# One hybrid decoder layer: part of the input projection as pairs of seven block products

## The chip, the cores and the metric

The kernel is one program on one core of a Trainium2 chip. The metric is the device time in microseconds, from launch to end. The engines are PE (TensorE, matrix products into eight PSUM banks), DVE (VectorE), ACT (ScalarE), POOL (GpSimd) and SP (SyncE, which here only issues DMAs). Each runs its own instruction list in order and waits on semaphores for the others.

## What is computed

One layer over 1024 tokens of width 1024: modulation from a conditioning vector, a token mixer with two kinds of linear-attention heads, and a squared-ReLU MLP, all in float32.

```
h = modulate(rms_norm(x), shift1, scale1)
proj = h @ w_in                      # 1024 x 3600
gq, gk, gv, g_lr, g_gate, hq, hf, hi, h_gate = split(proj)
# group A: 4 GLA heads (gq, gk, gv, low-rank gate), group B: 4 HGRN2 heads
forget = lb + (1 - lb) * sigmoid(hf)
o_hgrn = chunked_linear_attention(silu(hq), 1 - forget, hi, log(forget), 64)
mixed = concat(rms_norm(o_gla) * silu(g_gate), rms_norm(o_hgrn) * silu(h_gate))
x = x + gate1 * (mixed @ w_out)
h = modulate(rms_norm(x), shift2, scale2)
x = x + gate2 * (square(relu(h @ w_mlp1)) @ w_mlp2)
return rms_norm(x, final_norm_g)
```

A head's attention works on 16 chunks of 64 tokens. Its cumulative sums, exponentials, chunk states and outputs are what the code calls `cum`, `q_rel`, `k_rel`, `k_end`, `state` and `mixed`.

## The kernel before

Activations lie with features on the 128 partitions and tokens along the row: `a_hi` and `a_lo` hold eight tiles of 128 features by 1024 tokens. A float32 number is split into a rounded part and its remainder, so each product takes three matmuls of 512 columns: high weight by high activation, high by low, low by high.

The input projection is cut into units of 128 output columns. `half_unit` (called with the line 1338 of `product`) makes one unit for one half of the tokens: eight tiles times three matmuls, 24 in all, into one of four banks `UB`. Units 0 to 28 are the projection, the rest `w_out`. For each unit SP loads 512 KB (`load_unit`, into `raw`), ACT makes the high part (`high`, line 832), POOL the low part (`low`, line 721).

The units come in groups of four, and between the half-units PE does the attention of the head before (`attention_steps` gives the slots). The groups are `P0` (units 1 to 4) and `P1` (5 to 8) for pairs of GLA heads, `H0` (9 to 12) for the first HGRN head, three passes of `H1` (13 to 24) in a hardware loop for the others, and `G` (25 to 28) for the four HGRN gates. A head's group holds the columns HF, HQ, HI and GG in that order. While group `gi` runs on PE, DVE and ACT turn its columns into forget values, logarithms (`log_a`), the running sum (`cum`, line 2013), its two differences (lines 2015 and 2019), `k_rel` (2024), `k_end` (2026), `q_rel` (2037), `q_cum` (2050). The states (line 1941), masked scores (1921), norms (1949) and remainders of squares (1905) belong to the head before it. In the first groups DVE also adds up the modulation (`ada_acc`, line 1741), whose 48 tiles SP loads among the weights. ACT's function tables are swapped where a logarithm follows another function, as ACT_TABLE_LOAD shows.

The order on every engine is written out by hand. What an engine does first, it does first even if a later item is ready. PE may write a bank only after the reader of its last content has reported; `used` and `unit_read` hold that.

The MLP is already computed with the seven-product scheme of Strassen and Winograd, with weight sums by DVE (`weight_sum`, line 2124), weight remainders by POOL (line 777) and DVE (2145), and ready-made activation operands.

Of the kernel before, what the change touches and what calls it, by code (L numbers as in the profile page):

```python
# [21 lines left out]
F32 = mybir.dt.float32  # L22
# [21 lines left out]
U_OUT = 29  # L44
U_MLP = 37
# [16 lines left out]
BLOCK_ORDER = (3, 0, 1, 2)  # L62

# [92 lines left out]
def attention_steps(own, prev):  # L156
# [4 lines left out]
    s = [[] for _ in range(8)]  # L161
# [11 lines left out]
    if prev == "H":  # L173
        s[0] += [("k", 0, 0, 0)]
        s[1] += [("up", 0, 0, 2), ("up", 1, 0, 3), ("sc", 0, 0, 1)]
        s[2] += [("k", 0, 1, 0), ("sc", 0, 1, 1)]
        s[3] += [("o", 0, 0, 2)]
        s[4] += [("up", 2, 1, 3), ("up", 3, 1, 0), ("ss", 0, 0, 1)]
        s[5] += [("o", 0, 1, 2)]
        s[6] += [("ss", 0, 1, 3)]  # L180
# [5 lines left out]
    if own in "PH":  # L186
        s[7] += [("v", 0, 0, 0), ("v", 0, 1, 1)]
# [44 lines left out]
def chunks_after(prev, q):  # L232
# [7 lines left out]
IN_TURN = ((0, 0), (0, 1), (1, 0), (1, 1))  # L240
BY_HALVES = ((0, 0), (1, 0), (0, 1), (1, 1))
# [7 lines left out]
            for n in range(48)]  # L249


def hybrid_layer(nc, x, c, w_ada, b_ada, w_in, gate_w2, gate_b2, gla_g, lb_logits, hgrn_g, w_out, w1, w2,
# [3 lines left out]
    with ExitStack() as ctx:  # L256
# [61 lines left out]
        shift_gap = at("shift_gap", 206.6875, [P, KH])  # L318
        hid_dram = nc.dram_tensor("hidden_scratch", [4, 7, P, KH, HALF], F32, kind="Internal").ap()
# [75 lines left out]

        def tok(t, half):
            return t[:, half * HALF:(half + 1) * HALF]
# [14 lines left out]
        def at_chunk(pos):  # L412

            return chunked(cum)[:, :, pos:pos + 1].broadcast_to([P, NC, CH])
# [16 lines left out]
        MB = [[UB[2], UB[1], UB[0], UB[3]], [SB[0], SB[3], SB[1], SB[2]]]  # L431
        OB = (UB[2], UB[0], UB[3], UB[1])
# [35 lines left out]
        def groups(e, group):  # L468
# [4 lines left out]
            with e.Fori(1, 4) as h:  # L473
                group("H1", h + 2, h)
            group("G", 6, None)
# [38 lines left out]
        def _(sp):  # L514
# [44 lines left out]
            for j, q in enumerate(pair_cols + head_cols):  # L559
                load_unit(2 + j, j % 2, w_in, 0, q)  # L560
                for _ in range((2, 2, 5, 3, 4, 3, 3, 4, 2, 0, 0)[j]):
                    load_ada(n)
                    n += 1
            with sp.Fori(1, 4) as h:
                for j, q in enumerate(head_cols):
                    load_unit(4 * h + 9 + j, (1 + j) % 2, w_in, 0, h * P + q)
            for h in range(4):
                load_unit(25 + h, (1 + h) % 2, w_in, 0, HG + P * h)

            def load_out(v):  # L570

                if v >= 2:
                    sp.wait_ge(wlo_out, v - 1)
                else:
                    sp.wait_ge(wlo_ready, U_OUT + v - 1)
# [53 lines left out]
            for v in range(4):  # L629
# [1836 lines left out]
```

## Time and profile before

| | |
|---|---|
| median of three runs | 1174.47 us (1173.69 to 1175.45) |
| profiled execution, first to last instruction | 1173.7 us |
| PE busy | 1154.4 us, 98% |
| DVE, ACT, POOL busy | 807.6, 597.9, 444.0 us |
| stretch of the loop of heads and the gates on PE | 226.6 to 451.7 us |
| data moved | 152 MB |

The profile shows one execution, and its span lies 0.8 us under the median of the runs. In its rows a time is in us unless it is marked ns; "idle before" is time in which the engine waited, with the instruction that released it. The duration of a matmul includes its way through the array: matmuls overlap, and the pace of a series is the distance of their starts.

### The profile page before, as it was taken

Reading aid. Unit: us, or ns where it says so; the run is one execution under the profiler, and the core shown is the slowest. Engines: PE = TensorE matmul, PEld = TensorE weight load, DVE = VectorE, ACT = ScalarE, POOL = GpSimd, SP = SyncE. Lnnn points to the kernel's source line nnn. Section 1 sums busy time; section 2 is a strip of 40 time slices with the busy share of each in tenths; the row PEclk is TensorE's granted clock in tenths of the full one; section 3 lists DMA queues with packets and bytes.
Section 4 is the critical chain, followed back from the end, with each engine's and each line's share of the span. In section 5 each row is a group of like instructions: output and inputs, shape, how many; then the busy total and the mean of one; then the engine's idle time right before and its main releaser. Section 6 shows DMA issues by size and latency. Waiting matters only on the chain.

```text
span 1173.7 us, 15673 instructions
## 1 busy us (share of the span) xinstructions
PE 1154.4 (98%) x5651; PEld 958.1 (82%) x5651; DVE 807.6 (69%) x958; ACT 597.9 (51%) x899; POOL 444.0 (38%) x274
## 2 busy tenths in 40 slices
PE   7999999999999999999999999999999999999997
PEld 6788788888888888888888888888878888888886
DVE  6898766554536358367987755676796784966776
ACT  7763554646464647235655555455663443434325
POOL 1021111111111115326444442435367574666751
PEclk9899999999999999999999999999999999999999
DMA  9765241021111114341455435534723737437203
GB/s 351 261 224 171 90 145 36 18 55 36 36 36 36 37 38 143 90 161 72 117 171 165 158 118 171 179 135 130 220 72 118 251 98 253 151 123 280 92 1 144
DMA packets 148765, 152.02 MB, mean 130 GB/s; under 512 B 6228, under 2 KB 117976, under 8 KB 146008
## 3 DMA queue, kind: packets, MB, share of 16 engines
q1 hardware_dynamic: 148696, 151.12, 39.7%
q8 instruction: 41, 0.67, 0.2%
q14 instruction: 28, 0.23, 0.1%
HBM read 117.02 MB, written 34.08 MB: 129 GB/s over the span
## 4 chain that ended last, share of the span: by engine, by line
PE 91%; DVE 3%; issue 2%; DMA 2%; SPq 1%; ACT 1%; DVEq 0%; ACTq 0%
PE unit_bank L1338 33%; PE unit_bank L1640 8%; PE unit_bank L1642 8%; PE unit_bank L1641 8%; PE small_bank L1642 8%; PE small_bank L1640 8%; PE small_bank L1641 8%; PE small_bank L1338 3%; PE small_bank L1473 2%; DMA ada_slot<-in_w_ada_dram 2%; PE small_bank L1377 1%; PE small_bank L1465 1%; DVE ada_acc L1741 1%; DVE state L1941 1%; DVE op_lo L2254 0%
## 5 line engine op out<-in xcount | busy, mean ns | idle before, releaser
L777 POOL TENSOR_TENSOR wr_lo<-quarter,wr_hi 128x512 fp32r<-128x512 f32 x122 | 196.2, 1622 | 175.0 <-ACT wr_hi L1130 174.9
L1338 PE MATMUL unit_bank<-a_hi,w_hi 128*128 128x512 f32 x560 | 223.7, 400 | 0.0
L1338 PE MATMUL unit_bank<-a_hi,w_lo 128*128 128x512 f32 x560 | 218.7, 391 | 0.0
L1338 PE MATMUL unit_bank<-a_lo,w_hi 128*128 128x512 f32 x560 | 218.5, 390 | 0.0
L721 POOL TENSOR_TENSOR w_lo<-raw,w_hi 128x1024 fp32r<-128x1024 f32 x27 | 67.7, 2506 | 348.5 <-ACT w_hi L832 348.5
L1640 PE MATMUL unit_bank<-op_hi,wr_hi 128*128 128x512 f32 x452 | 176.6, 391 | 0.7 <-DVE op_lo L2254 0.6
L1642 PE MATMUL unit_bank<-op_hi,wr_lo 128*128 128x512 f32 x452 | 176.0, 389 | 0.0
L1641 PE MATMUL unit_bank<-op_lo,wr_hi 128*128 128x512 f32 x452 | 175.9, 389 | 0.0
L1640 PE MATMUL small_bank<-op_hi,wr_hi 128*128 128x512 f32 x448 | 174.6, 390 | 0.0
L1642 PE MATMUL small_bank<-op_hi,wr_lo 128*128 128x512 f32 x448 | 174.4, 389 | 0.0
L1641 PE MATMUL small_bank<-op_lo,wr_hi 128*128 128x512 f32 x448 | 174.4, 389 | 0.0
L1130 ACT ACTIVATE wr_hi<-wr_full 128x512 fp32r<-128x512 f32 x90 | 56.8, 631 | 176.2 <-DVE wr_full L2124 173.1
L2124 DVE TENSOR_TENSOR wr_full<-quarter,quarter 128x512 f32<-128x512 f32 x90 | 87.9, 977 | 57.6 <-PE unit_bank L1642 25.6
L1130 ACT ACTIVATE wr_hi<-quarter 128x512 fp32r<-128x512 f32 x136 | 82.7, 625 | 85.9 <-PE unit_bank L1642 47.4
L1338 PEld LDWEIGHTS unit_bank<-a_hi,w_hi 128*128 128x128 f32 x560 | 105.5, 188 | 23.0 <-issue 2.1
L1338 PEld LDWEIGHTS unit_bank<-a_hi,w_lo 128*128 128x128 f32 x560 | 105.4, 188 | 22.7
L1338 PEld LDWEIGHTS unit_bank<-a_lo,w_hi 128*128 128x128 f32 x560 | 105.6, 189 | 21.5 <-issue 0.7
L777 POOL TENSOR_TENSOR wr_lo<-wr_full,wr_hi 128x512 fp32r<-128x512 f32 x48 | 80.5, 1680 | 77.1 <-ACT wr_hi L1130 48.0
L1640 PEld LDWEIGHTS unit_bank<-op_hi,wr_hi 128*128 128x128 f32 x452 | 84.9, 188 | 19.0 <-issue 1.7
L1641 PEld LDWEIGHTS unit_bank<-op_lo,wr_hi 128*128 128x128 f32 x452 | 84.8, 188 | 17.8 <-issue 0.2
L1642 PEld LDWEIGHTS unit_bank<-op_hi,wr_lo 128*128 128x128 f32 x452 | 84.9, 188 | 17.7
L1641 PEld LDWEIGHTS small_bank<-op_lo,wr_hi 128*128 128x128 f32 x448 | 84.2, 188 | 17.5
(273 smaller groups left out, 1856.3 us busy)
## 6 DMA issues: line engine op xcount, KB each, us to landing
quarter<-in_w_mlp_dram SPq DMA_DIRECT2D x128, 256.0 KB, 4.4
hidden_scratch<-hid SPq DMA_DIRECT2D x98, 256.0 KB, 2.9
ada_slot<-in_w_ada_dram SPq DMA_DIRECT2D x48, 512.0 KB, 5.5
op_full<-hidden_scratch SPq DMA_DIRECT2D x21, 1024.0 KB, 4.9
raw<-in_w_in_dram SPq DMA_DIRECT2D x29, 512.0 KB, 3.8
raw<-in_w_out_dram SPq DMA_DIRECT2D x16, 512.0 KB, 4.0
x_stage<-in_x_dram SPq DMA_DIRECT2D x8, 512.0 KB, 5.1
x_scratch<-xT SPq DMA_DIRECT2D x2, 2048.0 KB, 8.3
```

The source lines that it names most:

```text
L721: pool.tensor_tensor(w_lo[slot][:, :, :], raw[slot][:, :, :], w_hi[slot][:, :, :].bitcast(F32), ALU.subtract).then_inc(wlo_ready, 1)
L777: pool.tensor_tensor(wr_lo[slot][:, :, :], split_source(n), wr_hi[slot][:, :, :].bitcast(F32), ALU.subtract).then_inc(wr_lo_pool, 1)
L1130: act.activation(wr_hi[slot][:, :, :], split_source(n), ACT.Copy).then_inc(wr_hi_ready, 1)
L1338: return pe.matmul(out_ap, left, right, start=start, stop=stop)
L1377: mm = pe.transpose(SB[b][:, i * P:(i + 1) * P], tile, ident[:, :])
L1465: pe.matmul(SB[b][:, i * P:(i + 1) * P], v_nat[:, which, 4 * half + i, :], masked[:, slot, i * P:(i + 1) * P], start=i == 0, stop=False, s ...
L1473: mm = pe.matmul(SB[b][:, c * CH:(c + 1) * CH], state[mine, n, :], q_cum[mine, n * CH:(n + 1) * CH], start=False, stop=c == 7, skip_group_ ...
L1640: pe.matmul(dst, wh, ah, start=opens, stop=False, skip_group_check=True)
L1641: pe.matmul(dst, wh, al, start=False, stop=False, skip_group_check=True)
L1642: mm = pe.matmul(dst, wl, ah, start=False, stop=k == KH - 1, skip_group_check=True)
L1741: dve.scalar_tensor_tensor(acc, src, col(cond, k), acc, ALU.mult, ALU.add).then_inc(ada_added, 1)
L2124: dve.tensor_tensor(dst[:, :, :], a[:, :, :], b[:, :, :], op).then_inc(w_sum, 1)
```

## The change

From the second HGRN head on (groups `H1` and `G`) the 16 units become 8 pairs of units. A pair is a matrix of two units by two halves of the features, multiplied with two halves of the features by two halves of the tokens, by seven block products instead of eight. A product has four tiles (12 matmuls). P1, P2, P6, P5, P4 and P3 run as wholes, P7 as four pieces of three matmuls between them.

- Activation sums are made once, in group `H0`, over xT's place after x has been stored to DRAM (8 DMAs): POOL does eight additions and subtractions and two remainders, each of 128x2048; ACT four high parts, DVE two remainders. The operand of P7 goes to DRAM and comes back for each pair in pieces.
- Weight sums of a pair: S3 and S2 by DVE, S1 and S4 by POOL. High parts by ACT (seven of 128x512 instead of two of 128x1024), low parts all by POOL.
- The results: ACT copies twice out of PSUM (`copy_part`), DVE does five additions (`join`) per pair. Columns are paired as (HQ, HF) and then (GG, HI) for a head.
- The hardware loop over three heads is written out. The order of the operations of a head on DVE and ACT is new, and PE's attention slots in it are nine instead of eight. The two half-units of unit 12 are swapped.
- Before `w_out`, x (4 MB) and one tile of `mixed` are loaded back. The first half of the output projection takes the tiles in another order, and the banks `MB` and `OB` change order.

The core of the diff:

```diff
@@ groups @@
-            with e.Fori(1, 4) as h:
-                group("H1", h + 2, h)
-            group("G", 6, None)
+            for h in range(1, 4):
+                paired(h + 2, h)
+            gates(6)
@@ gpsimd @@
-            for u in range(2, 13):
+            def add_parts(dst, k, half, n):
+                if n:
+                    pool.wait_ge(t_made, T_MADE_0 + n)
+                pool.tensor_tensor(dst[:, :, :], blocks(a_hi, k, half).bitcast(F32), blocks(a_lo, k, half).bitcast(F32), ALU.add
+                                   ).then_inc(t_made, 1)
...
+            for u in range(2, 10):
                 low(u, u % 2)
-            with pool.Fori(0, 4) as i:
-                for j in range(4):
-                    low(4 * i + 13 + j, (1 + j) % 2)
+            pool.wait_ge(x_out, X_OUT_0 + 16 * KT)
+            pool.wait_ge(lo_dve, 16)
+            add_parts(xs[1], 0, 1, 0)
+            add_parts(xs[0], 1, 1, 1)
+            subtract(xs[3], xs[0], xs[1], 2)
+            low(10, 0)
+            pool.wait_ge(t_high, T_HIGH_0 + 1)
+            pool.tensor_tensor(t3_lo[:, :, :], xs[3][:, :, :], t3_hi[:, :, :].bitcast(F32), ALU.subtract).then_inc(t_made, 1)
+            low(11, 1)
+            pool.wait_ge(t3_stored, T3_STORED_0 + 32)
+            add_parts(xs[2], 0, 0, 4)
+            subtract(xs[1], xs[1], xs[2], 5)
+            low(12, 0)
+            subtract(xs[3], xs[0], xs[1], 6)
+            add_parts(xs[0], 1, 0, 7)
+            subtract(xs[2], xs[0], xs[3], 8)
+            pool.wait_ge(t_high, T_HIGH_0 + 2)
+            pool.tensor_tensor(t1_lo[:, :, :], xs[1][:, :, :], t1_hi[:, :, :].bitcast(F32), ALU.subtract).then_inc(t_made, 1)
+            for p in range(PAIRS):
+                for prod in SPLIT_ORDER:
+                    if prod in (P5, P3):
+                        late_weight_sum(p, prod)
+                    pair_low(p, prod)
@@ scalar, group H0 @@
+                    act.wait_ge(t_made, T_MADE_0 + 9)
+                    act.activation(t1_hi[:, :, :], xs[1][:, :, :], ACT.Copy).then_inc(t_high, 1)
@@ scalar, paired @@
+                forget_tanh(0, early, "21")
+                output(0)
+                act.wait_ge(hk_ready, h + 1)
+                act.activation(t0[:, :], t0[:, :], ACT.Ln).then_inc(log_a, 1)
+                act.wait_ge(filled["sc"], before("sc", gi + 1))
+                tanh_of(q_rel, 1, early, "12")
+                pair_high(late, P6)
...
+                tanh_of(t0, 0, late, "11")
+                pair_high(late + 1, P1)
+                norm(1)
+                act.wait_ge(filled["o"], before("o", gi + 1))
+                value_of(1, late, "22")
+                pair_high(late + 1, P7)
+                pair_high(late + 1, P2)
+                value_of(0, late, "21")
@@ tensor @@
+            def seventh_piece(p, j):
+                if j == 0:
+                    pe.wait_ge(pair_lo, PAIR_LO_0 + split_of(p, P7))
...
+                        pe.wait_ge(c_read["12"], C_READ_0["12"] + p)
...
+                pair_product(early, P4)
+                attend(4)
+                pair_product(early, P3)
+                pair_product(late, P1)
+                attend(5)
+                seventh_piece(late, 0)
+                pair_product(late, P2)
...
+                pair_product(late, P4)
+                pair_product(late, P3)
+                if name == "H1":
+                    attend(8)
@@ vector, paired @@
+                join(early, "12")
+                dve.wait_ge(log_a, gi + 1)
+                dve.tensor_tensor_scan(own_cum[:, :], carry[:, :], t0[:, :], 0.0, ALU.mult, ALU.add).then_inc(cum_ready, 1)
+                dve.wait_ge(cum_ready, gi + 1)
+                dve.tensor_tensor(chunked(t0), chunked(own_cum), at_chunk(CH // 2 - 1, own_cum), ALU.subtract).then_inc(d_mid, 1)
...
+                dve.tensor_tensor(chunked(k_end), chunked(own_cum), at_chunk(CH - 1, own_cum), ALU.subtract).then_inc(d_last, 1)
+                silu_of(q_rel, 1, early, "12", made + 2)
+            def silu_of(dst, half, p, c, n):
+                dve.wait_ge(tanh_ready, TANH_0 + n)
+                wait_quarter(dve, p, c)
+                dve.scalar_tensor_tensor(tok(dst, half), tok(dst, half), 1.0, quarter_bank(p, c), ALU.add, ALU.mult).then_inc(c_read[c], 1)
@@ sync @@
+            load_out(0)
+            load_mixed_back()
+            load_out(1)
+            for i in range(2):
+                load_x_back(i)
+            for v in range(2, 4):
                 load_out(v)
```

## Rows read from the trace of the kernel before

**Rows 1.** The page: busy time of each engine, then the chain by engine.

```profile
PE 1154.4 (98%) x5651; PEld 958.1 (82%) x5651; DVE 807.6 (69%) x958; ACT 597.9 (51%) x899; POOL 444.0 (38%) x274
...
PE 91%; DVE 3%; issue 2%; DMA 2%; SPq 1%; ACT 1%; DVEq 0%; ACTq 0%
```

**Rows 2.** Stretch: us, busy PE, PEld, DVE, ACT, POOL, clock, DMA share, GB/s.

```profile
234.00:451.00 217.00, 216.53 (x1180) 181.75 (x1179) 111.51 (x142) 117.93 (x163) 42.71 (x19) 1.00 0.14 39
```

**Rows 3.** The chain of waits in that stretch: start us, us, what.

```profile
247.61 5.47 PE unit_bank L1338 x24
```

**Rows 4.** Timeline of POOL: start us, us, line, operation, [idle before and releaser].

```profile
145.71 2.40 POOL L721 TENSOR_TENSOR w_lo<-raw,w_hi 128x1024 fp32r<-128x1024 f32 x1 [11.50 <-ACT w_hi L832]
...
296.43 2.39 POOL L721 TENSOR_TENSOR w_lo<-raw,w_hi 128x1024 fp32r<-128x1024 f32 x1 [6.81 <-ACT w_hi L832]
```

**Rows 5.** Timeline of DVE in the same two places.

```profile
146.97 3.42 DVE L1741 SCALAR_TENSOR_TENSOR ada_acc<-ada_slot,misc,ada_acc 128x1024 f32<-128x1024 f32 x2
150.31 1.21 DVE L2037 SCALAR_TENSOR_TENSOR q_rel<-t,q_rel 128x1024 f32<-128x1024 f32 x1
...
156.65 1.30 DVE L1905 TENSOR_TENSOR sq_lo<-stat,sq_hi 128x512 fp32r<-128x512 f32 x2 [4.25 <-ACT sq_hi L1004]
...
174.76 0.70 DVE L2010 TENSOR_SCALAR t<-t 128x1024 f32<-128x1024 f32 x1
...
296.52 2.85 DVE L2010 TENSOR_SCALAR t<-t 128x1024 f32<-128x1024 f32 x1
```

**Rows 6.** POOL and DVE timelines in the MLP, both always with work.

```profile
623.97 1.74 POOL L777 TENSOR_TENSOR wr_lo<-quarter,wr_hi 128x512 fp32r<-128x512 f32 x1
624.48 1.77 DVE L2124 TENSOR_TENSOR wr_full<-quarter,quarter 128x512 f32<-128x512 f32 x1
625.67 1.74 POOL L790 TENSOR_TENSOR hid<-hid,hid1B 128x512 f32<-128x512 f32 x1
626.29 1.67 DVE L2124 TENSOR_TENSOR quarter<-quarter,wr_full 128x512 f32<-128x512 f32 x1
```

**Rows 7.** All instructions of POOL's line 777 in the trace: min/median/max ns.

```profile
L777 POOL TENSOR_TENSOR wr_lo<-quarter,wr_hi x122: 1271/1299/2987, 534.4 to 1128.6; 128x512 fp32r<-128x512 f32 x122
```

**Rows 8.** Timeline of PE at the end of P1 and in H0.

```profile
159.44 0.39 PE L1338 MATMUL small_bank<-sq_hi,ones 128*128 128x512 f32 x1
...
207.13 1.13 PE L1338 MATMUL small_bank<-v_nat,k_nat 64*128 64x256 f32 x6
```

**Rows 9.** Timeline of DVE in H0.

```profile
198.51 1.23 DVE L2019 TENSOR_TENSOR t<-cum 128x1024 f32<-128x1024 f32 x1 [4.04 <-ACT k_rel L1073]
199.66 1.22 DVE L2024 TENSOR_TENSOR k_rel<-k_rel,t 128x1024 f32<-128x1024 f32 x1
200.92 1.23 DVE L2026 TENSOR_TENSOR k_end<-k_end,t 128x1024 f32<-128x1024 f32 x1
```

**Rows 10.** Timeline of ACT in H0: it releases banks.

```profile
205.56 1.27 ACT L997 ACTIVATE stat<-small_bank,misc 128x512 f32<-128x512 f32 x2
```

**Rows 11.** Groups of DVE and ACT in one head, 302 to 359 us: busy us, mean ns.

```profile
L2013 DVE TENSOR_TENSOR_SCAN cum<-carry,t 128x1024 f32<-128x1024 uint8 x1 | 2.3, 2276 | 0.0
...
L1065 ACT ACT_TABLE_LOAD x1 | 1.3, 1283 | 0.0
```

**Rows 12.** Timeline of ACT: one norm of a head and its end.

```profile
331.51 1.28 ACT L997 ACT_TABLE_LOAD   x1
333.66 0.69 ACT L997 ACTIVATE stat<-small_bank,misc 128x512 f32<-128x512 f32 x1 [0.86 <-PE small_bank L1338]
...
336.20 1.07 ACT L957 ACTIVATE vT<-unit_bank 128x512 f32<-128x512 f32 x2
```

**Rows 13.** The page: DMA issues, KB each, median us to landing.

```profile
quarter<-in_w_mlp_dram SPq DMA_DIRECT2D x128, 256.0 KB, 4.4
...
x_scratch<-xT SPq DMA_DIRECT2D x2, 2048.0 KB, 8.3
```

**Rows 14.** A stretch near 48 us, columns as in rows 2.

```profile
48.00:50.00 2.00, 2.00 (x6) 1.55 (x5) 2.00 (x6) 2.00 (x4) 0.00 (x0) 0.50 1.10 384
```

More of the change, by code:

```diff
@@ L466, in h_place, with groups @@
             return (((P1, P2), (P6, P3))[half][k // KH], k % KH)
-        def groups(e, group):
+        def groups(group, paired, gates):
             group("P0", 0, None)
@@ new lines, in load_mixed_back, with load_x_back @@
+            def load_mixed_back():
+                sp.wait_ge(seventh_done, SEVENTH_0 + 4 * PAIRS - 1)
+                sp.dma_start(mixed[:, 0, :], mixed_dram).then_inc(mixed_back, 16)
+            def load_x_back(i):
+                sp.wait_ge(six_done, six_of(PAIRS - 1, P4 if i else P5))
+                for half in range(2):
+                    part = slice(half * HALF, (half + 1) * HALF)
+                    sp.dma_start(xT[:, 4 * i:4 * i + 4, part], x_dram[:, 4 * i:4 * i + 4, part]).then_inc(x_back[i][half], 16)
@@ L766, in _ @@
+            for half in range(2):
+                low_tiles(mixed, a_hi, a_lo, half)
+            pool.wait_ge(gated, 12)
             pool.memset(t1[:, :], 0.0).then_inc(sum2, 1)
@@ L1100, in inverse_rms @@
+            groups(group, paired, gates)
             def inverse_rms(half):
@@ L1566, in _, with stage @@
-            groups(pe, group)
+                    stage(name, steps[name][jj], used, gi, u0)
+            def stage(name, pieces, used, gi, u0):
+                prev = GROUPS[name][1]
+                older = {"P0": [], "P1": ["P0"], "H0": ["P1"], "H1": ["H0"] if gi == FIRST_PAIRED else ["H1"], "G": ["H1"]}[name]
+                both = []
+                for p in pieces:
+                    b = p[3]
+                    if name == "P0" and p[0] == "z" and p[2] == 1:
+                        half_unit(u0 + 1, 2, 0, a_hi, a_lo, tiles=range(KH))
+                    if b in used:
+                        pe.wait_ge(read[used[b][0]], reads(prev, used[b], gi))
+                    elif name == "P0":
+                        kind, count = (("ada", 3), ("ada", 4), ("ada", 1), ("ada", 2))[b]
+                        pe.wait_ge(read[kind], count)
+                    else:
+                        for name_ in older:
+                            kind = [q for x in steps[name_] for q in x if q[3] == b][-1][0]
+                            pe.wait_ge(read[kind], before("chunks" if kind == "up" else kind, gi))
+                    used[b] = p
+                    if p[0] not in ("sc", "up", "o"):
+                        step(prev, p, gi, u0)
+                        continue
+                    both.append(p)
+                    if len(both) == (2 if prev == "P" or p[0] == "up" else 1):
+                        {"sc": scores, "up": updates, "o": outputs}[p[0]](prev, both, gi)
+                        both = []
@@ L1568, in out_unit, with paired, gates @@
+            def paired(gi, h):
+                two_pairs("H1", gi)
+            def gates(gi):
+                two_pairs("G", gi)
+            groups(group, paired, gates)
             def out_unit(v):
@@ L2060, in scale_half @@
+            groups(group, paired, gates)
             def scale_half(half, k):
```

786 lines of the change are left out of this document (650 added, 136 removed).

## Prediction, made before the kernel was built

> **What bounds the kernel now.** I read the page first: PE is busy 98% of the span, and the chain that ended last is 91% PE [rows 1]. Then the stretch that the change rewrites, 226.6 to 451.7 us: of 217 us of it PE is busy 216.5, at the full clock, with POOL busy 43, DVE and ACT 112 and 118 [rows 2]. So matmuls taken out there are worth their whole time, and every new wait of PE costs its whole length. The chain of waits gives the pace: a half-unit of 24 matmuls takes 5.47 us [rows 3], 0.228 us each. The 32 half-units are 175 us of the 225; the other 50 are the attention of four heads, 12.6 us each. Last I read POOL beside DVE, since the change moves most of its preparation to POOL, and PE, DVE and ACT where PE has least slack.
>
> **What the change removes.** 16 units are 768 matmuls, 8 pairs of 7 products of 12 are 672. 96 x 0.228 = 21.8 us less on PE. Attention keeps its instructions, so this is the most that can be won: 5.5 us a head.
>
> **GpSimd against VectorE.** Two places show one rule. At 296.43 POOL starts a remainder of 2.39 us; DVE starts L2010 0.09 us later and takes 2.85 us, where the same instruction takes 0.70 at 174.76 [rows 4, 5]. It ended 0.55 after POOL. At 145.71 the same happens to an addition to `ada_acc`: the two take 3.42 us, 1 us too long [rows 4, 5]. Where both engines always have work they take turns: each DVE instruction of 0.69 takes 1.7, each of POOL's of 1.3 takes 1.74 [rows 6, 7]. So a DVE instruction with two operands in SBUF waits for the whole POOL instruction that is running, and POOL waits for DVE's. DVE instructions that read a PSUM bank show no such waiting in these views, so the new joins are safe. In the paired groups POOL's instructions are 1.3 us, and DVE loses up to 1.3 at each meeting. In H0 they are 128x2048, which this trace has none of. From 1.30 us at 512 columns and 2.40 at 1024 [rows 4, 7] each further 512 cost 1.1, so 2048 cost 4.6 us; bounds are 2.4 (no dearer than the longest seen) and 5.2 (four times 1.3). Ten of these are 46 us. The Trainium skill (GPSIMD Engine Reference, section 3.1) measures a `tensor_tensor` addition of 2048 fp32 elements at 4497 ns on GpSimd and 2293 on VectorE, and advises VectorE for elementwise work; by it the ten would be 45 us, and the change goes against that advice. No run here shows it yet.
>
> **End of P1, 7.6 us.** POOL is free after the weights of unit 9, at 148.1 us [rows 4], and x has long been stored: SP issues those eight DMAs near 105 us into an idle queue, so they cost nothing. POOL then runs three of the long instructions with no wait between. DVE has there, in order, the second addition to `ada_acc`, `q_rel`, five tiny ones and then the remainders of the squares, which begin at 156.65 and take 1.30 [rows 5]. Taking turns: POOL 149.2 to 153.8, addition to 155.0, POOL to 159.5, `q_rel` to 160.7, POOL to 165.2, the tiny ones, the remainders 166.1 to 167.4. PE wants the first sum of squares at 159.44 [rows 8] and gets it near 167. Bounds: 0 if POOL doesn't hold DVE, 9 if also the tiny ones are held singly. I take 7.6.
>
> **Middle of H0, 11.4 us.** After the store of P7's operand (2 MB, 8.3 us [rows 13], done near 197) POOL has six long ones and one of 2.4, of which five fall into the path of `k_end`. DVE's L2019, L2024 and L2026 run back to back before, 198.51 to 202.1 [rows 9]. With PE 8.2 us later, L2019 comes at 206.7 and waits 2.2, L2024 waits 4.6, L2026 4.6: 11.4 late. Behind L2026 stands ACT: it reads unit 10's banks, then the sums of squares at 205.56 [rows 10], and PE waits with the updates at 207.13 [rows 8] for exactly that bank. Before, the slack is 0.3 us, so all 11.4 go through. The swapped unit 12 waits for the same reads. Bounds 0 and 16.
>
> **First pair, 4 us.** ACT's high part of t1 waits for POOL's ninth result (226.2 us by the same turns), and behind it on ACT stand the squares, vT and the high parts of the first pair. The last reader of unit 12, which P2 waits for, comes after a norm (3.8 us without its wait [rows 12]). I get P2 about 4 us late; bounds 0 and 8.
>
> **Three heads, 16.5 us.** Steady state, two waits.
> First, piece 0 of the late P7 waits until DVE has read quarter 12 (`c_read["12"]`). Count from the end of the early P3. PE wants the piece after P1 (2.73) and the updates and sums (1.1 + 0.5 [rows 8]): at 4.1. The output bank is filled at -2.7; ACT takes three of 0.54 [rows 12] for it, a table load of 1.28 [rows 11] and the logarithm of 1.06: 1.2. DVE's scan takes 2.3 [rows 11], two differences 1.15 each as L2019 to L2024 [rows 9], the product 0.6: 6.5. That is 2.4 late, and 3.7 if POOL's low part of P6 falls between the differences, which it does by my count. I take 3.2.
> Second, the transposes of v. Count from the end of the late P6; PE is ready for them at 10.3. S4 on POOL comes behind a low part and a norm of DVE, done at 3.0. Only then may SP load the next first quarter (4.4 us [rows 13], 3.0 to 4.4 in this quiet queue): 6.7. ACT has that high part, a norm of 3.8, and four of 0.5 before it hands over the last half of v: 13.0. So 2.7 late. With 0.3 for P3, a head waits 6.2 us. My sums have attention at 12.1 us where it took 12.6 to 12.9, so 0.7 is absorbed: 5.5 a head, 16.5 for three. That eats the 5.5 that a head wins. Bounds 0 and 9 a head.
> The written-out loop takes branch gaps from DVE, none of which PE waits for: 0.
>
> **Gates and the way into w_out, 3.4 us.** The gates have no scan, and no wait of PE comes out at P7. But 4 MB of x and one tile of `mixed` come back ahead of the third and fourth `w_out` tile on one queue. At twice the 8.3 us for 2 MB [rows 13] they land 17 us after the last P5, unit 2 of `w_out` gets its weights 2.5 late, and the second 0.9. Bounds 0 and 8. New bank orders in the MLP change no count: 0.
>
> **Sum.** -21.8 + 7.6 + 11.4 + 4 + 16.5 + 3.4 = +21.1 us. On the profiled span of 1173.7 that is 1194.8, and with the 0.8 around it 1195.6 us.
>
> **Rivals.**
> A. The schedule holds: POOL's long instructions let DVE through and the two waits of a head are hidden; PE keeps its pace. For it: on average every engine has room (POOL 9 x 1.3 of 25 us a pair). Against: rows 4 to 6, and 0.3 us of slack in H0. Time 1174.5 - 21.8 = 1152.7, up to 1165 with small waits.
> B. Only POOL's hold in H0 is wrong (long instructions are cut into pieces, or POOL finds gaps): the heads still wait. 1174.5 - 21.8 + 16.5 + 3.4 + 3 = 1175.6, between 1168 and 1186.
> C. Slower still: PE's clock. After light use PE runs at 0.50 of its clock, 1.2 GHz, at 48 us: 6 starts in 2 us [rows 14], near 0.43 us a matmul instead of 0.228, 1.8 us for nine. If each of the three long waits and of some eight shorter ones is followed by that, it adds up to 11 x 1.8 = 20: 1205 to 1216. It decides from the point where a wait of PE is long enough to lower the clock; the stretches at full clock have none. The Trainium skill (TensorE: Matmul & The Clock Gate, "HAM oscillation") says that idle gaps between bursts send the array back to 1.2 GHz; by it the three long waits at least, 5 us, belong on top, 1200.6. No wait of several us stands in the trace to confirm it.
> That the kernel doesn't do what it says: 96 matmuls fewer is countable; if products were done anew, it would show as more matmuls. I give it nothing.
>
> **Chances.** Forecast (1186 to 1205) 0.44, A 0.16, B 0.22, C 0.16, outside 0.02. The range from 1167 to 1212 takes the forecast, B and most of C, and leaves A out. A measurement of this kernel can tell 0.2% from no change, 2.3 us. Faster by more (under 1172.1): A and a third of B, 0.23. Within: 0.09. Slower: 0.68.
>
> **What would show it.** Right: PE idle 7 us at the sums of squares near 159 us, with DVE's L1905 ending there; POOL instructions of 4.6 us; `k_rel` and `k_end` products of over 5 us in H0; in each head a gap of PE of 2 to 4 us ahead of the first P7 piece of the late pair, released by DVE's product on quarter 12, and one ahead of the v transposes, released by ACT. Wrong: DVE's two-operand instructions of 1.2 us beside a long POOL one; PE without gaps between 226 and 440 us. The prediction fails most easily at the hold of the long instructions (19 us of it rest on it), next at the order in which ACT gets through a head.

## Result and profile after

The changed kernel takes 1220.89 us (median of four runs, 1216.72 to 1222.83) where the kernel before takes 1174.5: the ratio is 1.0394, 95% interval 1.0374 to 1.0414. It is slower, by 46 us where 21 were forecast, and it lies above the predicted range (1212). The profiled execution spans 1219.2 us, 45.5 more than before.

The page, busy time by engine with the number of instructions, and the shares of the chain that ended last (compare [rows 1]):

```profile
PE 1155.1 (95%) x5555; PEld 952.6 (78%) x5555; DVE 884.2 (73%) x1023; ACT 621.4 (51%) x939; POOL 560.4 (46%) x340
...
PE 79%; DVE 7%; issue 4%; ACT 4%; DMA 3%; POOL 2%; SPq 1%; DVEq 0%; ACTq 0%; POOLq 0%
```

These two lines already hold the result. PE has the 96 matmuls less that were promised (5651 to 5555), worth 21.8 us, and yet it is busy 0.7 us longer: 22.5 us went mostly into slower matmuls. The clock accounts for 20.6 of them: from the first wait on PE is busy for 41.1 us while the granted clock is at the lower of its two levels, and half of such time is lost (0.43 us a matmul for 0.228); the kernel before is never busy at that level behind 60 us. The other 1.9 us are not placed. PE's idle time, span less busy, grew from 19.3 to 64.1 us: 44.8. So 45.5 = 44.8 of waits + 22.5 of slower matmuls - 21.8.

By stretch (us, then busy PE, PEld, DVE, ACT, POOL, the granted clock, DMA share, GB/s), to be held against [rows 2]:

```profile
161.00:175.00 14.00, 9.30 (x40) 7.83 (x41) 11.63 (x15) 6.93 (x10) 3.56 (x2) 0.76 0.35 112
...
200.00:240.00 40.00, 30.45 (x175) 23.89 (x171) 28.10 (x27) 17.96 (x23) 28.46 (x7) 0.87 0.11 34
...
325.00:387.00 62.00, 56.18 (x295) 46.37 (x296) 39.73 (x52) 35.23 (x52) 26.51 (x19) 0.92 0.37 115
387.00:448.00 61.00, 55.05 (x280) 45.39 (x278) 39.34 (x51) 35.09 (x52) 25.66 (x19) 0.92 0.35 102
448.00:490.00 42.00, 41.98 (x237) 35.40 (x236) 30.39 (x45) 25.88 (x40) 21.06 (x16) 1.00 0.52 165
```

The loss sits at the end of P1, in H0, in the first pair and in each of the heads. The gates (448 to 490) run without a wait and at the full clock. A head takes 61.2 us (transposes of v at 315.24, 376.34, 437.72) where it took 56.6 (282.36, 338.90, 395.49).

**The first head.** POOL and DVE at the end of P1, and POOL with DVE in H0 (compare [rows 4, 5, 9]):

```profile
147.49 11.08 POOL L976 TENSOR_TENSOR x_sum<-a_hi,a_lo 128x2048 f32<-128x2048 f32 x2
158.65 5.36 POOL L982 TENSOR_TENSOR x_sum<-x_sum,x_sum 128x2048 f32<-128x2048 f32 x1
...
183.68 4.63 POOL L1013 TENSOR_TENSOR t_lo<-x_sum,t_hi 128x2048 fp32r<-128x2048 f32 x1 [6.84 <-ACT t_hi L1299]
```

```profile
154.01 5.64 DVE L2557 SCALAR_TENSOR_TENSOR q_rel<-t,q_rel 128x1024 f32<-128x1024 f32 x1
159.57 4.45 DVE L2334 TENSOR_TENSOR misc<-misc 128x4 f32<-128x4 f32 x1
164.06 0.18 DVE L2335 RECIPROCAL misc<-misc 128x4 f32<-128x4 f32 x1
...
208.65 5.62 DVE L2544 TENSOR_TENSOR k_rel<-k_rel,t 128x1024 f32<-128x1024 f32 x1
214.20 5.54 DVE L2546 TENSOR_TENSOR k_end<-k_end,t 128x1024 f32<-128x1024 f32 x1
```

A product of DVE that takes 1.2 us takes 5.6 beside POOL's long instructions, and one of four columns takes 4.45, until POOL's third sum ends at 164.0. PE's timeline shows the two waits (in brackets, with the releaser) and what follows the second (compare [rows 8]):

```profile
165.70 0.77 PE L1775 MATMUL small_bank<-sq_hi,ones 128*128 128x512 f32 x1 [6.70 <-DVE sq_lo L2448]
...
224.51 2.04 PE L1775 MATMUL small_bank<-v_nat,k_nat 64*128 64x256 f32 x6 [9.30 <-ACT stat L1268]
226.48 1.97 PE L1814 MATMUL small_bank<-ident,ada_acc 128*128 128x128 f32 x8
228.10 0.77 PE L1775 MATMUL unit_bank<-a_hi,w_hi 128*128 128x512 f32 x1
228.67 0.63 PE L1775 MATMUL unit_bank<-a_lo,w_hi 128*128 128x512 f32 x1
229.10 0.63 PE L1775 MATMUL unit_bank<-a_hi,w_lo 128*128 128x512 f32 x1
```

After the wait the updates take 2.04 us instead of 1.13 and matmuls start 0.43 us apart instead of 0.23; the granted clock from 224 to 230 us is 0.50, 1.2 GHz, the lower of the two levels.

**The heads.** DVE and PE at the P7 piece of the first paired head:

```profile
284.85 2.29 DVE L2713 TENSOR_TENSOR_SCAN cum<-carry,t 128x1024 f32<-128x1024 uint8 x1
287.18 1.23 DVE L2715 TENSOR_TENSOR t<-cum 128x1024 f32<-128x1024 f32 x1
288.32 2.29 DVE L2718 TENSOR_TENSOR k_end<-cum 128x1024 f32<-128x1024 f32 x1
290.54 0.68 DVE L2632 SCALAR_TENSOR_TENSOR q_rel<-q_rel,unit_bank 128x512 f32<-128x512 f32 x1
```

```profile
291.32 0.47 PE L2056 MATMUL unit_bank<-piece_x,pw_hi 128*128 128x512 f32 x1 [3.22 <-issue]
```

The chain of waits just before the transposes of v (start, us, what):

```profile
302.81 1.31 POOL pw_full L993
...
304.14 4.29 DMA pair_quarter<-in_w_in_dram
...
308.51 0.63 ACT pw_hi L1359
...
309.16 1.28 ACT L1389
...
312.46 0.63 ACT stat L1391
...
314.61 0.50 ACT vT L1419
...
315.24 1.34 PE small_bank L1814 x8
```

All PE waits over 0.2 us between 100 and 520 us make 44.3 us (the rows are rounded one by one):

| place, prediction's step | measured | in the sum |
|---|---|---|
| end of P1 | 6.7 | 7.6 |
| middle of H0 | 9.3 | 11.4 |
| first pair (0.26, 1.76, 4.14, 1.70) | 7.9 | 4 |
| three heads: P7 pieces 3 x 3.2, transposes of v 2.5, 2.6, 2.7 | 17.5 | 16.5 |
| way into w_out (0.56, 0.52, 1.88) | 3.0 | 3.4 |
| matmuls slower than 0.228 us | 22.5 | 0 |

The sum of the waits was forecast to within 1.4 us (42.9), in part by luck, since the first pair came out 3.9 us too long and H0 2.1 too short; the heads, the largest term, were right to 1 us. Nearly the whole miss is the last line.

### The profile page after: what moved, and what is told of

The parts are those of the page before. It is cut to its first block, busy times and chain, and to the rows that moved or that the text cites. A ratio compares the mean times of both kernels' runs of the same rounds, so it can differ in the third digit from the quotient of the medians.

```text
span 1219.2 us, 15677 instructions
## 1 busy us (share of the span) xinstructions
PE 1155.1 (95%) x5555; PEld 952.6 (78%) x5555; DVE 884.2 (73%) x1023; ACT 621.4 (51%) x939; POOL 560.4 (46%) x340
## 4 chain that ended last, share of the span: by engine, by line
PE 79%; DVE 7%; issue 4%; ACT 4%; DMA 3%; POOL 2%; SPq 1%; DVEq 0%; ACTq 0%; POOLq 0%
PE unit_bank L1775 14%; PE unit_bank L2181 8%; PE unit_bank L2183 8%; PE unit_bank L2182 8%; PE small_bank L2181 8%; PE small_bank L2183 8%; PE small_bank L2182 8%; PE small_bank L1775 2%; PE unit_bank L2036 2%; PE unit_bank L2037 2%; PE unit_bank L2038 2%; POOL pw_lo L1001 2%; DVE ada_acc L2282 1%; DMA ada_slot<-in_w_ada_dram 1%; PE small_bank L1912 1%
## 5 line engine op out<-in xcount | busy, mean ns | idle before, releaser
L1775 PE MATMUL unit_bank<-a_hi,w_hi 128*128 128x512 f32 x304 | 122.9, 404 | 1.9 <-DVE w_lo L2426 1.9
L1775 PE MATMUL unit_bank<-a_lo,w_hi 128*128 128x512 f32 x304 | 119.9, 394 | 0.0
L1775 PE MATMUL unit_bank<-a_hi,w_lo 128*128 128x512 f32 x304 | 119.6, 393 | 0.0
L2181 PEld LDWEIGHTS small_bank<-op_hi,wr_hi 128*128 128x128 f32 x448 | 84.1, 188 | 17.5 <-POOL wr_lo L1043 0.2
L2183 PEld LDWEIGHTS small_bank<-op_hi,wr_lo 128*128 128x128 f32 x448 | 84.1, 188 | 17.6
L936 POOL TENSOR_TENSOR w_lo<-raw,w_hi 128x1024 fp32r<-128x1024 f32 x11 | 27.7, 2515 | 121.5 <-ACT w_hi L1098 121.5
L1001 POOL TENSOR_TENSOR pw_lo<-pair_quarter,pw_hi 128x512 fp32r<-128x512 f32 x32 | 48.7, 1522 | 72.5 <-ACT pw_hi L1359 72.5
```

Of the source, the lines that this page charges most:

```text
L936: pool.tensor_tensor(w_lo[slot][:, :, :], raw[slot][:, :, :], w_hi[slot][:, :, :].bitcast(F32), ALU.subtract).then_inc(wlo_ready, 1)
L1001: pool.tensor_tensor(pw_lo[place][:, :, :], pair_source(prod), pw_hi[place][:, :, :].bitcast(F32), ALU.subtract).then_inc(pair_lo, 1)
L1775: return pe.matmul(out_ap, left, right, start=start, stop=stop)
L2181: pe.matmul(dst, wh, ah, start=opens, stop=False, skip_group_check=True)
L2183: mm = pe.matmul(dst, wl, ah, start=False, stop=k == KH - 1, skip_group_check=True)
```

## Experiments

The theory is the table: DVE held behind POOL's instructions, two waits in every head by the order on DVE and on ACT, and behind every wait a stretch at the lower clock. The rivals are named with each run. The span is that of the profiled execution. "Idle" is the span less PE's busy time; "slow" is busy time less 1154.4 plus 0.2275 us for every matmul fewer than 5651. It holds the price of the lower clock and 1.5 to 5 us besides, and it comes from one execution.

| kernel | median us | ratio to before (95%) | span | idle | slow |
|---|---|---|---|---|---|
| changed | 1220.9 | 1.0394 (1.0374 to 1.0414) | 1219.2 | 64.1 | 22.5 |
| 1 sums in column tiles | 1209.2 | 1.0308 (1.0291 to 1.0326) | 1204.5 | 53.0 | 18.9 |
| 2 sums in halves, a single execution | 1214.2 | | 1212.5 | 61.8 | 18.1 |
| 3 added matmuls in the waits | 1208.2 | 1.0305 (1.0286 to 1.0324) | 1206.1 | 50.2 | 9.0 |
| 4 ScalarE's order | 1210.5 | 1.0307 (1.0282 to 1.0331) | 1208.7 | 59.7 | 16.4 |
| 5 VectorE's order | 1220.2 | 1.0402 (1.0385 to 1.0419) | 1217.6 | 62.2 | 22.8 |
| 6 VectorE's order and states | 1221.5 | 1.0419 (1.0401 to 1.0436) | 1218.2 | 65.4 | 20.2 |
| 7 P2 ahead of the P7 piece | 1216.4 | 1.0380 (1.0361 to 1.0398) | 1211.5 | 61.1 | 17.8 |
| 8 runs 1, 4, 6 together | 1196.8 | 1.0204 (1.0187 to 1.0221) | 1196.8 | 49.8 | 14.4 |
| 9 runs 1, 4 together | 1197.2 | 1.0204 (1.0187 to 1.0221) | 1196.5 | 48.4 | 15.5 |
| 10 as 9, P2 ahead of the P7 piece | 1196.3 | 1.0207 (1.0189 to 1.0225) | 1193.4 | 50.2 | 10.6 |
| 11 as 9, added matmuls | 1195.0 | 1.0182 (1.0165 to 1.0199) | 1193.8 | 39.6 | 10.7 |

Differences of a few us need care. The kernel before was run again beside every set: its median was 1174.5 us beside the changed kernel and 1172.7 to 1173.3 beside the others, so across sets the ratios are the fair measure. By them runs 1, 3 and 4 gained 10.1, 10.4 and 10.2 us where the medians give 11.7, 12.7 and 10.4. And PE reaches its first wait, ahead of which no edit has changed its work, between 157.0 and 159.0 us in these profiles: before 60 us it is busy at the lower clock for 6.8 us in the changed kernel and in runs 1, 4 and 6, for 3.4 in 5, 7, 8 and 9, for 10.2 in 11 and not at all in 2, 3 and 10. So what a run changed is read from its own stretch.

### 1. GpSimd's ten long instructions in column tiles

```diff
-                pool.tensor_tensor(dst[:, :, :], a[:, :, :], b[:, :, :], ALU.subtract).then_inc(t_made, 1)
+                for j in range(KH):
+                    ins = pool.tensor_tensor(dst[:, j, :], a[:, j, :], b[:, j, :], ALU.subtract)
+                ins.then_inc(t_made, 1)
```

> The ten GpSimd instructions of 128x2048 are issued as four of 128x512 each; everything else is as changed. Theory (a VectorE instruction with two SBUF operands waits for the whole GpSimd instruction in front of it): each turn costs VectorE 1.3 us instead of 4.6, so PE's gap of 6.7 us at the sums of squares near 159 us falls under 2, that of 9.3 us near 215 us under 4, and with the slow matmuls behind them 13 to 17 us are won: 1204 to 1208 us. Rival (what counts is GpSimd's work as a whole, not the length of one instruction): the sums take as long or longer, and the time stays within 3 us of 1220.9.

Measured 11.7 us less where 13 to 17 were expected: the theory's direction, 1.2 us above its range. DVE in this kernel, at the two places shown above:

```profile
149.45 2.28 DVE L2561 SCALAR_TENSOR_TENSOR q_rel<-t,q_rel 128x1024 f32<-128x1024 f32 x1
151.65 1.25 DVE L2338 TENSOR_TENSOR misc<-misc 128x4 f32<-128x4 f32 x1
...
163.38 1.26 DVE L2573 COPY decay<-cum 128x16 f32<-128x16 f32 x1
...
202.13 2.30 DVE L2548 TENSOR_TENSOR k_rel<-k_rel,t 128x1024 f32<-128x1024 f32 x1
204.35 2.30 DVE L2550 TENSOR_TENSOR k_end<-k_end,t 128x1024 f32<-128x1024 f32 x1
```

The same work on the same data in shorter instructions holds DVE 1.1 us at a time, not 4.4. The wait near 159 us falls from 6.7 to 0.99, the one in the middle of H0 from 9.3 to 2.68, with a new one of 1.81 at 181.6. What is left over in the first pair (2.44, 4.02, 0.85) and in the heads stays. So the hold is by instruction, and these waits were its doing. The COPY at 163.38 has one operand and 16 columns and takes 0.17 us in the changed kernel (at 168.47); here, beside POOL's third sum, it takes 1.26. So some instructions with one operand are held too.

### 2. The same ten in halves

```diff
-                for j in range(KH):
-                    ins = pool.tensor_tensor(dst[:, j, :], a[:, j, :], b[:, j, :], op)
+                for j in range(0, KH, 2):
+                    ins = pool.tensor_tensor(dst[:, j:j + 2, :], a[:, j:j + 2, :], b[:, j:j + 2, :], op)
```

> The ten long GpSimd instructions as two of 128x1024 each. PE's gap near 159 us was 6.7 us with 128x2048 and 1.0 us with 128x512. Theory (a VectorE instruction waits for one GpSimd instruction, here 2.4 us): about 3 us there, with a time between 1209 and 1221 us, near 1213. Rival (the hold is not set by the length of one instruction): a gap like one of the two others.

For 2048, 1024 and 512 columns the wait in H0 is 9.3, 5.3 and 2.7 us (at 1024 with a further one of 2.4 at 228.1), but the one at the end of P1 is 6.7, 6.2 and 1.0. That is a miss: 3 us were expected there, and the rival had it, a gap like that of the whole sums. Only the time (1214.2 for some 1213, from one execution) came as expected. DVE and POOL of this kernel say why:

```profile
149.92 3.38 DVE L2561 SCALAR_TENSOR_TENSOR q_rel<-t,q_rel 128x1024 f32<-128x1024 f32 x1
153.22 2.37 DVE L2338 TENSOR_TENSOR misc<-misc 128x4 f32<-128x4 f32 x1
155.62 0.18 DVE L2339 RECIPROCAL misc<-misc 128x4 f32<-128x4 f32 x1
155.84 2.08 DVE L2340 TENSOR_TENSOR misc<-misc 128x4 f32<-128x4 f32 x1
157.96 0.17 DVE L2342 TENSOR_SCALAR misc<-misc 128x4 f32<-128x4 f32 x1
158.16 2.18 DVE L2343 TENSOR_TENSOR misc<-misc 128x4 f32<-128x4 f32 x1
160.38 3.40 DVE L2452 TENSOR_TENSOR sq_lo<-stat,sq_hi 128x512 fp32r<-128x512 f32 x2
```

```profile
157.98 4.64 POOL L974 TENSOR_TENSOR x_sum<-x_sum,x_sum 128x1024 f32<-128x1024 f32 x2
```

DVE has seven instructions with two SBUF operands there, three of them of four columns, and each waits for one of POOL's. Whole sums (three) or halves (six) both last DVE until POOL is done, at 164.0 and 162.6; with twelve quarters DVE gets through first. In these three kernels the price of holding is about the smaller of POOL's remaining work and DVE's instructions times POOL's length. In H0 only three of DVE's stand in the path, so there the length decides.

### 3. Matmuls without use in the two waits of a head

```diff
                 attend(5)
+                if name == "H1":
+                    pe.wait_ge(read["o"], before("o", gi) + 1)
+                    keep_warm(2, 12)
                 seventh_piece(late, 0)
...
                 if name == "H1":
+                    pe.wait_ge(read["up"], before("chunks", gi) + 15)
+                    keep_warm(0, 9)
                     attend(8)
```

`keep_warm` issues matmuls of 512 columns into a bank that is free and isn't read before it is overwritten.

> In each of the three heads PE does 12 extra matmuls of 512 columns ahead of the first P7 piece of the late pair and 9 ahead of the v transposes, into a bank that is free there, with results that nobody reads. They fill 2.7 of the 3.2 us and 2.0 of the 2.5 us that PE waits. Theory (a wait costs its length and then a run of matmuls at half clock, which the trace shows as 6 to 12 starts 0.43 us apart): the waits stay where they end, the slow runs behind them go, 10 to 14 us less: 1207 to 1211 us. Rival (the slow matmuls have another cause, and PE's work in the gap only adds): 1221 us or more.

PE does 63 matmuls more and the kernel is 12.7 us faster. The page, PE at the P7 piece, and the stretches of the last two heads:

```profile
PE 1155.9 (96%) x5618; PEld 954.1 (79%) x5618; DVE 882.4 (73%) x1023; ACT 620.7 (51%) x939; POOL 560.7 (46%) x340
```

```profile
286.24 2.90 PE L2071 MATMUL small_bank<-a_hi,ones 128*128 128x512 f32 x12
289.66 0.47 PE L2056 MATMUL unit_bank<-piece_x,pw_hi 128*128 128x512 f32 x1 [0.52 <-issue]
```

```profile
325.00:387.00 62.00, 60.49 (x328) 50.47 (x328) 40.22 (x54) 36.66 (x54) 28.87 (x20) 1.00 0.40 122
387.00:448.00 61.00, 59.56 (x327) 49.72 (x326) 42.05 (x55) 35.67 (x52) 27.61 (x19) 1.00 0.39 119
```

The clock is 1.00 where it was 0.92. In the changed kernel PE is busy for 24.7 us at the lower level between 290 and 445 us, in the three heads; here it never is, and half of that, 12.4 us, is what the clock cost there, most of the 16.4 that three seven-product heads save. The rest agrees: the added matmuls take 14.3 us and the waits in the heads shrink by 13.0, so that a head should be 3.7 us shorter, and it takes 57.5 us instead of 61.2. "Slow" falls by 13.5 over the whole kernel, but part of that lies before 60 us, where nothing was edited.

### 4. ScalarE's order: the norm ahead of a high part that waits for a load

```diff
-                pair_high(late + 1, P1)
                 norm(1)
+                pair_high(late + 1, P1)
```

> ScalarE does the second norm of a head ahead of the high part of the next pair's P1, which waits for a load. Theory (the chain S4 on GpSimd, load of 4.3 us, high part, norm of 3.8 us, copies of v holds PE's v transposes): the load is now hidden by the norm, the three gaps of 2.6 us and the slow matmuls behind them go, 4 to 4.5 us a head, 1207 to 1209 us. Rival (the copies are late because ScalarE has too much to do, not because it waits for the load): under 3 us in all.

10.4 us less, 1.5 us above the expected range. The wait at v falls from 2.5 to 2.7 us to 1.33 in each head, and "slow" by 6.1. The predicted chain (S4, load, high part, norm, v) is confirmed in part: take the load out from before the norm, and half the wait goes, where all of it was expected to. The rest hangs on ACT's high part of P1, POOL's low part, DVE's second sum and the addition before v's last copy: four steps on three engines.

### 5. VectorE's order: quarter 12 directly behind the scan

```diff
+                silu_of(q_rel, 1, early, "12", made + 2)
                 dve.wait_ge(cum_ready, gi + 1)
                 dve.tensor_tensor(chunked(t0), chunked(own_cum), at_chunk(CH // 2 - 1, own_cum), ALU.subtract).then_inc(d_mid, 1)
...
                 dve.tensor_tensor(chunked(k_end), chunked(own_cum), at_chunk(CH - 1, own_cum), ALU.subtract).then_inc(d_last, 1)
-                silu_of(q_rel, 1, early, "12", made + 2)
```

> VectorE reads quarter 12 (the product for q_rel) right after the running sum and ahead of the two differences. Theory (the first P7 piece of the late pair waits for that read alone): the three gaps of 3.2 us and the slow matmuls behind them go, 5 us a head, about 1205 us. Rival (the piece waits for GpSimd's low part of P6, which the chain of waits names in front of it): the gaps stay and the time is 1221 us.

A miss: 0.7 us, which is nothing (ratios 1.0402 and 1.0394). The waits at P7 are gone, and three of 2.69 to 2.79 us stand at the outputs with the states, which DVE's line 2659 releases behind the same two differences:

```profile
287.57 2.32 DVE L2719 TENSOR_TENSOR k_end<-cum 128x1024 f32<-128x1024 f32 x1
...
290.94 2.64 DVE L2659 SCALAR_TENSOR_TENSOR state<-state,decay,small_bank 128x128 f32<-128x128 f32 x7
```

```profile
293.63 3.68 PE L1912 MATMUL small_bank<-q_cum,state 128*128 128x64 f32 x16 [2.69 <-DVE state L2659]
```

The outputs then take 3.68 us at the low clock where 2.00 us are shown for them at the high one in run 10 below, so that the clock costs as much as before ("slow" 22.8 for 22.5).

### 6. The states moved forward too

```diff
                 dve.tensor_tensor(chunked(t0), chunked(own_cum), at_chunk(CH // 2 - 1, own_cum), ALU.subtract).then_inc(d_mid, 1)
+                states(1)
...
                 dve.tensor_tensor(k_rel[:, :], k_rel[:, :], t1[:, :], ALU.mult).then_inc(k_rel_ready, 1)
-                states(1)
```

> As the run before with quarter 12 read right after the running sum, and now the second half of the states stands between the two differences instead of behind the product for k_rel. In that run the wait at the P7 piece was gone, but PE waited 2.7 us for those states at the outputs of the second half. Theory (two waits stood behind one another, the second hidden by the first): both go now, 3 x (3.2 + some 2 of slow matmuls), 1203 to 1207 us. Rival (a third wait of the same size stands behind, since VectorE is short of time in this half of a head): 1215 to 1221 us.

The rival had it: 1221.5. Both waits are gone; new ones of 3.16, 1.29 and 3.15 us stand at the second sum of squares, one of 1.54 behind the transfer of a P7 piece, and those of v grow to 3.66 and 4.56 (the third is 1.93). The reading that fits is that DVE as a whole is behind PE at this point of a head and that its order only chooses who waits; no run took work away from DVE, so it isn't shown by itself.

### 7. On PE, P2 of the late pair ahead of the first P7 piece

```diff
-                seventh_piece(late, 0)
                 pair_product(late, P2)
+                seventh_piece(late, 0)
                 seventh_piece(late, 1)
```

> The changed kernel with the new place of P2 alone (P2 of the late pair ahead of the first P7 piece). Theory of the single wait: 3 x 1.8 us of waits and 3 x (1.5 to 2.4) us of slow matmuls go, if the transposes of v don't take it: 1209 to 1212 against 1220.9. Rival: in the changed kernel the transposes of v stand behind ScalarE, whose norm waits for the high part of P1's next sum and that for a transfer (4.3 us), a chain that starts from PE's progress only in part; PE then waits 4 us instead of 2.6 there and two thirds of the gain are lost: 1216 to 1220.

1216.4: the rival had the time (1216 to 1220), if not quite the place. By the medians that is 4.5 us less, by the ratios 1.6 with overlapping intervals, so a gain is not shown. In the profile, an execution at the fast end (1213.5), the P7 waits fall from 3.2 to 0.53 us, but the outputs with the states wait 1.64 and v 2.7 to 3.0, where the rival had all of it at v: of 8.1 us of idle time 5.6 come back in the heads. It is "slow" that falls more, by 4.7.

### 8. Runs 1, 4 and 6 in one kernel

The edits of runs 1, 4 and 6, and in H0 ACT's two copies of the tanh ahead of t4's high part:

```diff
-                    act.wait_ge(t_done, T_DONE_0 + 1)
-                    act.activation(t4_hi[:, :, :], xs[2][:, :, :], ACT.Copy).then_inc(t_high, 1)
                     act.wait_ge(q_cum_ready, gi + 1)
                     tanh_and_copy(3, (1, 0))
+                    act.wait_ge(t_done, T_DONE_0 + 1)
+                    act.activation(t4_hi[:, :, :], xs[2][:, :, :], ACT.Copy).then_inc(t_high, 1)
```

> The GpSimd sums as four instructions of 128x512, the norm of ScalarE ahead of the high part of P1, VectorE's order as in e5, and unit 12 read ahead of the high part of t4. Theory (waits and the slow matmuls behind them are separate places on PE's path, so their shares add): 11.7 + 10 + 15 + 3 us off 1220.9: 1178 to 1184 us. Rival (they share slack on ScalarE and VectorE, so one mended place gives way to the next): 1190 us or more.

The rival again: 1196.8, as the shares don't add. The first pair shows 2.46, 2.27 and 3.47 us, the last one now behind the transfer of a P7 piece; the second sums of squares still wait 3.04, 1.31 and 3.12.

### 9. The same without VectorE's new order

> The combined version without the new order of VectorE's instructions: GpSimd's ten long instructions in column tiles, ScalarE's norm(1) ahead of the high part of P1's last sum, and the two copies of the tanh ahead of t4's high part. Additive shares of the single runs: 1220.9 - 11.7 (tiles) - 10.4 (ScalarE's order) = 1198.8. Theory: VectorE's new order only moves a wait of about 3 us from the P7 piece to the second sum of squares, where it is as long and leaves PE's clock lower, so the version without it is level with the combined one (1196.8) within 3 us: 1195 to 1200. Rival: the new order did gain in company of the other edits (its own run stood 0.7 us under the changed kernel, and its wait at P7 is gone), then this version stands 5 us or more above, at 1202 to 1206. What the trace tells: the P7-piece waits are back at 3.2 us in each head and the second sum of squares has none over 0.6.

Runs 1 and 4 with run 8's order of the high part of t4. 1197.2: level with run 8, as the theory said, and the P7 waits are back at 3.2 us. The single shares of runs 1 and 4, 11.7 and 10.4, predicted 1198.8: these two add, to 2 us. VectorE's order is worth nothing in company either.

### 10. Run 9 with P2 ahead of the P7 piece

> GpSimd's sums in column tiles and ScalarE's new order (the version of 1197.15 us), and on PE the product P2 of the late pair ahead of the first piece of P7 instead of behind it: the 2.7 us of P2 lie in the wait for VectorE's product on quarter 12. Count in that version's trace: PE is free at 276.40; P2's low weights are ready at 277.83 (GpSimd 275.72 + 2.11) and ScalarE has read its bank at 276.4, so PE waits 1.4 us instead of 3.2; P2 ends at 280.6, VectorE has read quarter 12 at 279.5, so that P7 follows without a wait. Waits of 1.3 to 1.4 us stood with no slow matmuls behind them in that trace (300.90), so the 1.2 to 1.6 us of slow matmuls behind each P7 piece go as well. Theory: 3 x (1.8 + 1.4) = 9.6 us less, 1186 to 1190. Rival: the rest of the head is bound by ScalarE's and VectorE's own chains, so that PE, coming 3.2 us earlier to the transposes of v or to the second sum of squares, waits there for what it gained: 1194 to 1198, with waits there grown by 2 to 3 us.

The medians differ by 0.9 us with overlapping runs, so the rival holds. The piece waits 0.51 us, and then DVE's states are what PE meets:

```profile
279.66 0.47 PE L2060 MATMUL unit_bank<-piece_x,pw_hi 128*128 128x512 f32 x1 [0.51 <-issue]
...
283.80 2.00 PE L1916 MATMUL small_bank<-q_cum,state 128*128 128x64 f32 x16 [1.62 <-DVE state L2663]
```

With 1.33 to 2.07 us ahead of v, the heads wait 12 us in all where they waited 13.7.

### 11. Run 9 with added matmuls in the waits

Twelve ahead of the P7 piece and four ahead of v in each head, placed as in run 3.

> The version before this one in the list, with 12 added 512-column matmuls ahead of the P7 piece and 4 ahead of the transposes of v in each head (48 more matmuls that compute nothing that is used, 48 x 0.228 = 10.9 us of PE at full clock against waits of 3.2 and about 1.5 us in each head, 14 us). Theory of the clock: the waits in the heads shrink to under 1 us and the slow matmuls behind them go; from the version beside it 3 x (about 2.5 us of slow wide matmuls and small ones) less the fillers' overshoot comes off, 5 to 9 us: 1190 to 1194 if that one is at 1198. Rival: the slow stretch is a property of the work behind the waits (products that read tiles written only then) and not of the clock; then the fillers only add and the time is that of the version beside it or 1 to 3 us more. The other waits, in the first head and the first pair, stay, so that neither expects the time of the kernel before (1173).

2.2 us less where 5 to 9 were expected. A head takes 56.1 us against 57.4 in run 9, three of them 3.9, but the piece of P7 ahead of the heads comes 1.9 us later from its transfer. PE is busy at the lower level for 10.0 us in the three heads of run 9 and not at all here: 5.0 us of clock where the theory had 7.5, because the waits of 1.3 us at v had no slow matmuls behind them, and the added matmuls take 1.1 us more than the waits lose. The theory's sign holds, its size doesn't.

No version beats the kernel before. The best, run 11, is 21 us above it; its 39.6 us of idle time are still 20 more than before's 19.3.

## Why the prediction was wrong

**What held.** PE bounds this stretch, and each wait costs its length: the count of matmuls fell by 96, and the waits appeared at the places named, each with the releaser named, except that the P7 piece's is read from DVE's timeline (product done at 291.22, piece at 291.32) since the profile puts it down to issue. In numbers: end of P1 6.7 for 7.6, H0 9.3 for 11.4, P7 3.2 for 3.2, v 2.6 for 2.7, w_out 3.0 for 3.4. POOL's 128x2048 takes 4.63 us alone, for an estimate of 4.6; the Trainium skill (GPSIMD Engine Reference, section 3.1) gives 4497 ns, and the trace agrees. POOL takes 5.4 to 5.6 where it waits its turn behind DVE. The rule "two operands in SBUF" was read partly from the wrong instruction: L2010, a TENSOR_SCALAR of 128x1024, has one, and went from 0.70 to 2.85 us all the same [rows 5]. In the heads of the changed kernel it takes 1.67. No term of the sum hung on it.

**The failed step: the clock stood beside the sum, not in it.** The prediction treated the forecast's waits and rival C's clock as alternatives, and its sum priced the lower clock at nothing. But C's only condition is that waits come and are long enough, and the forecast itself asserted eleven of them, three of 4 to 11 us. Both are true at once: 45.5 = 21.1 forecast + 1.9 more idle time (44.8 for the sum's 42.9) + 22.5, of which 20.6 are the clock's. With C's own price of 20 in the sum it would have been 1215.6. C's range ended at 1216 and the record at 1212, as the waits' bounds and the clock's were never added. The argument that no long wait stood in the trace to confirm it was no reason for zero: the row at 48 us [rows 14] showed what the level costs, and the stretch at full clock had no waits to show anything. Nor did the level need a long wait. Ahead of that row, from 38 us on, no wait of PE was over 0.5 us; what stood there were such short waits and sixteen matmuls of one column:

```profile
44.87 1.87 PE L1338 MATMUL small_bank<-ones,ada_acc 128*128 128x1 f32 x16
46.61 0.63 PE L1338 MATMUL unit_bank<-a_hi,gate_w 128*128 128x512 f32 x1
```

The Trainium skill (TensorE: Matmul & The Clock Gate, "HAM oscillation") says that gaps between bursts bring back 1.2 GHz; the trace agrees, as the granted clock is 0.62 from 291 to 295 us, behind a wait of 3.2. The 5 us that the prediction made of that rule was four times too small, since shorter waits count too: PE's busy time at the lower level prices at 6.5 us behind the three long waits (6.7, 9.3, 4.1) and at 14 behind the seven of 1.9 to 3.2. Run 3 is the proof that it is the clock and not the work behind the waits: the same products in the three heads, with the waits filled, run at 1.00.

**Mis-sized terms.** The first pair was 7.9 for 4 (within its bounds, 0 to 8): only t1's lateness was counted (4.14), neither the bank that P1 and the k_end transposes wait for (1.76) nor the first P7 piece's transfer (1.70). H0's waits were 2 us shorter, since L2539 (L2019 before) was held 1.0 us, not 2.2, and POOL's smaller part fell elsewhere. In the heads the 0.7 us that were to be absorbed were not, and P3 has no wait. Two slips of the working are small: PE was taken to come 8.2 us late to H0 where the step before had 7.6, and 2.73 + 1.1 + 0.5 is 4.3, not 4.1.

**Where the size per wait was off.** C had 11 x 1.8. Measured are ten runs of slow wide matmuls between 166 and 520 us, 76 in all, 1.5 us each, 14.8 together; of the other 7.7 some 6 are short matmuls such as the updates and transposes at 224.5, which C left out. In a head the period is 56.6 - 5.5 + 5.8 of waits = 56.9 by the sum and 61.2 measured: 4.3 us more, on 5.8 us of waits, of which the clock is 4.1 (24.7 us of busy time at the lower level in three heads, halved).

**What stays open.** Why the same wait is sometimes followed by more slow matmuls than at other times: the three P7 waits of 3.2 us had 8, 11 and 12 behind them in the changed kernel and 6, 8 and 8 in run 9, and in run 10 one of 1.64 us had seven behind it and one of 2.07 none. A seven-product kernel with a shorter DVE path per head (joins or differences on another engine) wasn't tried.

## What to carry to other kernels

On an engine that bounds the kernel, price a new wait at its length plus a stretch at the lower clock (here some 20 us on 44.8, nearly half as much again), and put that in the sum, not among the rivals. Work moved to GpSimd is charged to every VectorE instruction with two SBUF operands that meets it, however small, and to some with one (a COPY and a TENSOR_SCALAR here): keep GpSimd's instructions short, and count VectorE's, not their columns. Reordering may only move a wait to the next reader: it did so with VectorE's order twice and with PE's, while ScalarE's new order, which let a norm run during a transfer, took half of one away.

## What was not expected of the hardware

- A `tensor_tensor` of four columns on DVE (some 0.16 us) takes 4.45 us beside a POOL instruction of 128x2048, 2.1 to 2.4 beside 128x1024, 1.0 to 1.25 beside 128x512. A RECIPROCAL or TENSOR_SCALAR of four columns with one operand takes 0.17 to 0.18 while the 128x1024 ones run (run 2), but a COPY of 16 columns took 1.26 for 0.17 (run 1) and a TENSOR_SCALAR of 1024 columns 2.85 for 0.70 [rows 5]. What tells the two kinds apart isn't shown here.
- 63 matmuls whose results nobody reads made the kernel 12.7 us faster by the medians (10.4 by the ratios), because they kept the granted clock in the heads at 1.00 instead of 0.92.
- A wait moved from wide matmuls to small ones cost as much clock in run 5: sixteen output matmuls took 3.68 us instead of 2.00.
